# Last stage of a layer kernel: sixteen tokens per partition, loads at the last scatter's landing, four tiles through TensorE

## What is computed

```python
x = x + g1 * rmsnorm(y, norm_post_mix[l])          # called x1 in the kernel
h = rmsnorm(x, norm_pre_ffn[l]) * (1.0 + sc2) + sh2
out = hier_moe(tokens, ...)                        # sum of two experts' rows per token, called ys
x = x + g2 * rmsnorm(out, norm_post_ffn[l])        # the last stage
```

## Time and profile before

| | |
|---|---|
| median of 3 runs | 2342.1 us (2340.84 to 2342.71) |
| the profiled execution | 2340.58 us, its span 2338.9 us |
| mean granted TensorE clock | 0.97 of 2.4 GHz |
| busy share of the span | PE 93%, DVE 60%, ACT 45%, POOL 28% |
| barrier at the end of the experts | 2291.9 us |
| first square, last sum of the last stage | 2296.2 us, 2335.7 us |

### The profile page before, as it was taken

How to read it: one execution, slowest core, us unless ns; L and a number is a source line. 1 busy time by engine, 2 the same in 40 slices (tenths; PEclk the granted TensorE clock), 3 DMA queues, 4 the chain that set the end, 5 groups by cost and what they waited for, 6 DMA issues and landing times. The chain is left out here.

```text
span 2338.9 us, 35385 instructions
## 1 busy us (share of the span) xinstructions
PE 2166.2 (93%) x11602; PEld 1828.4 (78%) x11603; DVE 1401.5 (60%) x2035; ACT 1056.0 (45%) x1518; POOL 651.5 (28%) x648
## 2 busy tenths in 40 slices
PE   8999999999999679997999959999999999999990
PEld 5888888899998668886888847778788888887770
DVE  6322222387654578886566654765767665647876
ACT  4422322243322036664332234755666665547763
POOL 0000000000000658886222232332333333222323
PEclk9999999999999989998999979999999999999995
DMA  8632333546551986665563336998988987868997
GB/s 308 243 102 109 127 151 130 192 156 215 175 172 63 354 327 229 228 220 190 169 214 138 117 117 183 344 291 250 338 261 261 282 269 246 251 173 277 350 351 301
DMA packets 297516, 518.78 MB, mean 222 GB/s; under 512 B 33406, under 2 KB 206022, under 8 KB 292664
## 3 DMA queue, kind: packets, MB, share of 16 engines
q1 hardware_dynamic: 271000, 439.52, 54.9%
q0 software_dynamic: 17216, 44.60, 8.5%
q10 hardware_dynamic: 9216, 33.56, 3.6%
HBM read 397.28 MB, written 129.09 MB: 225 GB/s over the span
## 5 line engine op out<-in xcount | busy, mean ns | idle before, releaser
L2573 DVE TENSOR_TENSOR e_w_low<-e_w_whole,e_w_high 128x2048 fp32r<-128x2048 f32 x192 | 431.1, 2287 | 92.9 <-ACT e_w_high L2525 92.2
L2525 ACT ACTIVATE e_w_high<-e_w_whole 128x2048 fp32r<-128x2048 f32 x192 | 357.6, 1914 | 47.7 <-DMA e_w_whole<-in_moe_w_down_dram 23.7
L2464 PE MATMUL e_pG<-e_w_high,e_xT 128*128 128x512 f32 x768 | 300.0, 391 | 1.2 <-ACT e_xT L2518 1.2
L2465 PE MATMUL e_pG<-e_w_low,e_xT 128*128 128x512 f32 x768 | 299.7, 390 | 0.0
L859 PE MATMUL proj_acc<-w_high,hT_high 128*128 128x512 f32 x672 | 263.9, 393 | 0.0
L859 PE MATMUL proj_acc<-w_low,hT_high 128*128 128x512 f32 x672 | 262.0, 390 | 0.0
L859 PE MATMUL proj_acc<-w_high,hT_low 128*128 128x512 f32 x672 | 261.8, 390 | 0.0
L2473 PE MATMUL e_pY<-e_w_high,e_hT 128*128 128x512 f32 x768 | 225.4, 405 | 17.5 <-ACT e_hT L2537 17.5
L2468 PE MATMUL e_pG<-e_w_high,e_xT 128*128 128x512 f32 x768 | 189.9, 389 | 0.0
L2473 PEld LDWEIGHTS e_pY<-e_w_high,e_hT 128*128 128x128 f32 x768 | 138.2, 190 | 45.6 <-ACT e_hT L2537 20.3
L2464 PEld LDWEIGHTS e_pG<-e_w_high,e_xT 128*128 128x128 f32 x768 | 144.8, 189 | 31.7 <-issue 1.6
(11 more groups left out here) (304 smaller groups left out, 4171.3 us busy)
## 6 DMA issues: line engine op xcount, KB each, us to landing
e_w_whole<-in_moe_w_gate_dram SPq DMA_DIRECT2D x64, 1024.0 KB, 8.2
e_w_whole<-in_moe_w_up_dram SPq DMA_DIRECT2D x64, 1024.0 KB, 11.1
e_w_whole<-in_moe_w_down_dram SPq DMA_DIRECT2D x64, 1024.0 KB
by_token<-tok SPq DMA_DIRECT2D x32, 512.0 KB, 3.0
w_in_raw<-in_w_mod_dram SPq DMA_DIRECT2D x32, 512.0 KB, 4.3
m_tok<-by_token SPq DMA_DIRECT2D x16, 768.0 KB, 5.4
s_kv<-by_token SPq DMA_DIRECT2D x20, 512.0 KB, 5.8
modulated_high<-hT_high SPq DMA_DIRECT2D x9, 1024.0 KB, 3.9
```

The lines of the kernel that those rows point to most:

```text
L2464: nc.tensor.matmul(pG[:, half], xT[:, 0, k], wh[:, half, w], start=(k == 0), stop=False)
L2465: nc.tensor.matmul(pG[:, half], xT[:, 0, k], wl[:, half, w], start=False, stop=False)
L2525: nc.scalar.activation(wh[:, third, part], raw[:, third, part], ACT.Copy).then_inc(whs.sem, 1)
L2573: nc.vector.tensor_tensor(wl[:, third, part], raw[:, third, part], wh[:, third, part].bitcast(F32), ALU.subtract).then_inc(wls.sem, 1)
```

## The change

- Tile t now holds the tokens 16p + t, p being the partition, so that a partition's 16 rows lie one behind the other in memory. `by_rows` makes that view of `ys`, of x1 and of the output. Any set of neighbouring tiles is then one DMA.
- x1 is loaded with 4 DMAs (2 MB each) in place of 16; SyncE does not wait for them, VectorE and TensorE do.
- `c_yy` gets its place ahead of the stage, where the split weights lay. SyncE issues the loads of `ys` at the end of its program in the experts, when GpSimd reports the last scatter landed (`summed_up`): 6 DMAs of 1, 1, 2, 4, 4 and 4 tiles.
- The output goes out in 7 DMAs.
- The tiles 2, 6, 10 and 14 (`by_pe`) are not summed by VectorE. ScalarE makes a diagonal matrix of rstd (`finish`); TensorE adds ident times x1 (done at the stage's start) and the diagonal times the tile in PSUM, in two halves of 512 columns, all in f32; ScalarE copies the sum into `c_yy`. `finish(t - 3)` stands behind the square of tile t for t = 5, 9 and 13, and `finish(14)` at the end.

```diff
--- before.py
+++ after.py
@@ -2264,6 +2264,7 @@
     with ExitStack() as st:
         raw = g["e_raw"]
         kit.fill("e_fill_first", 2048, st)
+        g["c_yy_at"] = nc.sbuf_base
         wh = kit.sb("e_w_high", [P, 3, THIRD], F32R, stack=st)
         wl = kit.sb("e_w_low", [P, 3, THIRD], F32R, stack=st)
         ids = kit.sb("e_ids", [P, IDS], I32, stack=st)
@@ -2301,7 +2302,10 @@
         ya = kit.counter("e_y_act", 1, credit=3)
         yd = kit.counter("e_y_dve", 1, credit=3)
         junk = kit.counter("e_paused")
-        x1_early = kit.landing("c_x1_early_in", dmas=NL)
+        g["x1_early"] = x1_early = kit.landing("c_x1_early_in", dmas=4)
+        g["c_y_in"] = kit.landing("c_y_in", len(LOADS))
+        summed_up = kit.counter("c_rows_summed")
+        g["c_yy"] = kit.at("c_yy", [P, NL, D], g["c_yy_at"])
         block = st.enter_context(nc.Block())
 
         def over_blocks(eng, body, enter=None):
@@ -2349,17 +2353,19 @@
             sp.wait_ge(x_in.sem(0), x_in.at(0))
             with sp.Fori(1, NE // 4) as e:
                 load(e)
-            for t in range(EARLY, NL):
-                sp.dma_start(early_x1(g, t), dram["x1"][t]).then_inc(x1_early.sem(0), 16)
+            sp.dma_start(g["x1_rest"][:], by_rows(dram["x1"].rearrange("t p d -> (t p) d"), EARLY, NL)).then_inc(x1_early.sem(0), 16)
             with sp.Fori(NE // 4, NE) as e:
                 load(e)
 
             for third in range(3):
 
                 sp.wait_ge(wls.sem, wls.at(NE - 1, 2 * third + 2))
-                for t in range(4 * third, 4 * third + 4):
-                    sp.dma_start(early_x1(g, t), dram["x1"][t]).then_inc(x1_early.sem(0), 16)
-            sp.wait_ge(x1_early.sem(0), x1_early.at(0))
+                to = raw[:, third].rearrange("p (t d) -> p t d", t=4)
+                sp.dma_start(to, by_rows(dram["x1"].rearrange("t p d -> (t p) d"), 4 * third, 4 * third + 4)).then_inc(x1_early.sem(0), 16)
+
+            sp.wait_ge(summed_up.sem, summed_up.at(0))
+            for n, (t, last) in enumerate(LOADS):
+                sp.dma_start(g["c_yy"][:, t:last], by_rows(dram["ys"][0:SEQ], t, last)).then_inc(g["c_y_in"].sem(n), 16)
 
         @block.gpsimd
         def _(pool):
@@ -2428,6 +2434,7 @@
                 nc.gpsimd.tensor_copy(held[:, 0:3 - n], held[:, 1:4 - n]).then_inc(held_on.sem, 1)
                 scatter(b + n)
                 landed(b + n)
+            pool.sem_inc(summed_up.sem, 1)
             pool.wait_ge(x_in.sem(0), x_in.at(b))
             pool.sem_inc(junk.sem, 1)
 
@@ -2604,6 +2611,13 @@
 
 
 EARLY = 12
+LOADS = ((0, 1), (1, 2), (2, 4), (4, 8), (8, 12), (12, 16))
+STORES = ((0, 2), (2, 4), (4, 8), (8, 12), (12, 14), (14, 15), (15, 16))
+
+
+def by_rows(rows, t, last):
+
+    return rows.rearrange("(p t) d -> p t d", t=NL)[:, t:last]
 
 
 def early_x1(g, t):
@@ -2618,34 +2632,63 @@
     GROUP = 2
 
     with ExitStack() as st:
-        yy = kit.sb("c_yy", [P, NL, D], stack=st)
+        kit.fill("c_fill_first", 2048, st)
+        assert nc.sbuf_base == g["c_yy_at"]
+        kit.sb("c_yy_room", [P, NL, D], stack=st)
+        yy = g["c_yy"]
         sq = kit.sb("c_sq", [P, D], stack=st)
         ss = kit.sb("c_ss", [P, 2, NL], stack=st)
-        y_in = kit.landing("c_y_in", NL)
-        o_out = kit.landing("c_out", dmas=NL)
+        diag = kit.sb("c_diagonal", [P, NL // 4, P], stack=st)
+        pS = kit.ps("c_sums", [P, NL // 4, 2, 512], st)
+        y_in = g["c_y_in"]
+        x1_early = g["x1_early"]
+        o_out = kit.landing("c_out", dmas=len(STORES))
         ssq = kit.counter("c_ssq")
         eps_added = kit.counter("c_eps_added")
         rstd = kit.counter("c_rstd")
         gained = kit.counter("c_rows_gained")
+        diags = kit.counter("c_diagonal_ready")
+        summed = kit.counter("c_sums_ready")
         outs = kit.counter("c_out_ready")
+        outs_pe = kit.counter("c_out_of_sums_ready")
         block = st.enter_context(nc.Block())
+
+        def by_pe(t):
+
+            return t % 4 == 2
+
+        def before(t, kind):
+
+            return sum(by_pe(n) == kind for n in range(t))
 
         @block.sync
         def _(sp):
-            for t in range(NL):
-                sp.dma_start(yy[:, t], dram["ys"][t * P:(t + 1) * P, :]).then_inc(y_in.sem(t), 16)
-            for t in range(NL):
-                sp.wait_ge(outs.sem, outs.at(t))
-                sp.dma_start(io["out0"][0, t * P:(t + 1) * P, :], yy[:, t]).then_inc(o_out.sem(0), 16)
+            to = by_rows(io["out0"].rearrange("o n d -> (o n) d"), 0, NL)
+            for t, last in STORES:
+                sp.wait_ge(outs.sem, before(last, False))
+                if before(last, True):
+                    sp.wait_ge(outs_pe.sem, before(last, True))
+                sp.dma_start(to[:, t:last], yy[:, t:last]).then_inc(o_out.sem(0), 16)
             sp.wait_ge(o_out.sem(0), o_out.at(0))
 
         @block.scalar
         def _(act):
-            for t in range(NL):
-                act.wait_ge(y_in.sem(t), y_in.at(0))
-                if t:
-                    act.wait_ge(ssq.sem, ssq.at(t - 1))
-                nc.scalar.activation(sq[:], yy[:, t], ACT.Square, accum_out=ss[:, 0, t:t + 1]).then_inc(ssq.sem, 1)
+            def finish(t):
+                n = before(t, True)
+                act.wait_ge(rstd.sem, rstd.at(t // GROUP))
+                nc.scalar.activation(diag[:, n], g["ident"][:, :], ACT.Copy, scale=ss[:, 1, t:t + 1]).then_inc(diags.sem, 1)
+                act.wait_ge(summed.sem, summed.at(n))
+                nc.scalar.activation(yy[:, t], pS[:, n].rearrange("p a b -> p (a b)"), ACT.Copy).then_inc(outs_pe.sem, 1)
+
+            for n, (t0, last) in enumerate(LOADS):
+                act.wait_ge(y_in.sem(n), y_in.at(0))
+                for t in range(t0, last):
+                    if t:
+                        act.wait_ge(ssq.sem, ssq.at(t - 1))
+                    nc.scalar.activation(sq[:], yy[:, t], ACT.Square, accum_out=ss[:, 0, t:t + 1]).then_inc(ssq.sem, 1)
+                    if t >= 5 and by_pe(t - 3):
+                        finish(t - 3)
+            finish(NL - 2)
 
         @block.gpsimd
         def _(pool):
@@ -2654,6 +2697,22 @@
                 span = slice(n * GROUP, (n + 1) * GROUP)
                 rstd_root(nc, g, pool, eps_added, n, 1, ss[:, 1, span], ss[:, 0, span], D).then_inc(rstd.sem, 1)
 
+        @block.tensor
+        def _(pe):
+            pe.wait_ge(x1_early.sem(0), x1_early.at(0))
+            for t in range(NL):
+                if by_pe(t):
+                    for h in range(2):
+                        nc.tensor.matmul(pS[:, before(t, True), h], g["ident"][:, :], early_x1(g, t)[:, h * 512:(h + 1) * 512], start=True, stop=False)
+            for t in range(NL):
+                if by_pe(t):
+                    n = before(t, True)
+                    pe.wait_ge(gained.sem, gained.at(t))
+                    pe.wait_ge(diags.sem, diags.at(n))
+                    for h in range(2):
+                        m = nc.tensor.matmul(pS[:, n, h], diag[:, n], yy[:, t, h * 512:(h + 1) * 512], start=False, stop=True)
+                    m.then_inc(summed.sem, 1)
+
         @block.vector
         def _(dve):
             def gain(t):
@@ -2662,9 +2721,12 @@
 
             for t in range(GROUP):
                 gain(t)
+            dve.wait_ge(x1_early.sem(0), x1_early.at(0))
             for t in range(NL):
                 if t + GROUP < NL:
                     gain(t + GROUP)
+                if by_pe(t):
+                    continue
                 dve.wait_ge(rstd.sem, rstd.at(t // GROUP))
                 dve.wait_ge(gained.sem, gained.at(t))
                 nc.vector.scalar_tensor_tensor(out=yy[:, t], in0=yy[:, t], scalar=ss[:, 1, t:t + 1], in1=early_x1(g, t), op0=ALU.mult, op1=ALU.add).then_inc(outs.sem, 1)
```

## The result

The changed kernel takes 2347.5 us (median of 20 runs, 2344.4 to 2351.4), the kernel before 2342.4 (20 runs beside it): ratio 1.0019, 95% interval 1.0011 to 1.0027, so about 4.4 us slower (the medians lie 5.1 apart). Run again later (e10_again) it gave 1.0014 (1.0004 to 1.0023). The difference is small, but the interval leaves out 1, so it is a measured one. The profiled execution took 2351.39 us, its span 2349.4.

A forecast was written before the change was run, and what follows sets the result against it. VectorE was taken to set the kernel's end; after the change ScalarE's chain of squares, finishes, root and tail would end at 2341.3 against 2338.9, +2.4 us. On the median 2342.1 + 2.4 = 2344.5 us, range 2337.5 to 2350.

The forecast's parts named there:

- The early loads: Last stage: loads issued at about 2287.5, ScalarE starts 4.1 us earlier; SyncE being held bounded at +1.3 on tile 4.
- The group of tile 4: Last stage: tiles 4 to 7 land together at 2300.6; ScalarE waits for tile 4 until then, not 2297.1.
- One finish: ScalarE's diagonal 0.47, TensorE's products 3.8, PSUM copy 1.03, handovers 0.15: 5.45 us at the lower clock, 3.7 at the higher.
- The clock: TensorE in the last stage: higher clock (2.4 GHz) for the first finish, lower (1.2 GHz) for the other three.
- lower clock for the first as well: Rival: TensorE at the lower clock for the first finish too; +1.75, so +4.2, 2346.3 us; chance 0.2.
- the higher one throughout: Rival: TensorE stays at the higher clock, all four finishes at 3.7 us; -2.8, 2339.3 us; chance 0.2.
- The last root: GpSimd's root for the last pair, ahead of the finish of tile 14: 2.25 us, done at 2332.2.
- The tail: Behind the last PSUM copy: 3.2 us of store and end, plus 0.4 for tile 15's store issued behind tile 14's.
- Strided rows: Rival, loads of `ys`: reads 64 KB apart run at half rate, ending at 2353, +14; chance 0.05.
- The packets of x1: Rival: 16 KB packets of x1 land the last-but-one scatter 4.3 us later, the last scatter 1.2 later; chance 0.15.
- Hidden, at nothing: x1 in 4 DMAs instead of 16, ahead of the last stage: costs no time, save for the rival on packets.
- "Below" the forecast: Range's lower end, 2337.5: all finishes at the higher clock less 2 us for earlier landings; over 0.2% faster had chance 0.1.

The follow-up runs named there:

- e10_again: The changed kernel as it is, run once more: stage 61.97 us, ratio 1.0014 (1.0004 to 1.0023) to the kernel before.
- e3_early_only: The kernel before with only its sixteen tile loads of `ys` issued early, in the old layout: stage 61.09 us, ratio 1.0011 to the kernel before.
- e7_loads_by_tile: The changed kernel with its early loads of `ys` as 16 DMAs of one tile: stage 66.25 us, one execution, 2350.34 us.
- e2_pe_busy: The changed kernel with six unread TensorE products behind each of the first three sums: stage 56.72 us, ratio 1.0002 to the kernel before.
- e4_apart: The changed kernel with each PSUM copy four squares behind its diagonal, and tiles 1, 5, 9, 13 by TensorE: stage 54.38 us, ratio 0.9974 to before.

## Why the prediction held, and which steps did not

Forecast 2344.5 us with a range of 2337.5 to 2350, no measurable change the likeliest. Measured 2347.5; the last stage +2.65 us where +2.4 was forecast. "No measurable change" is not what came out: I took 0.2% as the least that can be told, but the interval is 0.08% to either side, and 1.0019 is a real loss. It lies within the 0.2% that I gave the best chance. That the stage is so near is luck in part. Tile 4 (0.7 us) and the finishes of tiles 2 and 14 (0.4 and 0.3) came in under the forecast, the roots (0.6 at the last one, 0.3 net at the two before) and the tail (0.7) over it. The working against the trace, in us behind TensorE's end in the experts:

| step | forecast | measured |
|---|---|---|
| loads of `ys` issued | 7.9 | 7.78 |
| first square | 12.4 | 12.66 |
| tile 4 begun | 21.0 | 20.28 |
| finish of tile 2 over | 27.1 | 25.96 |
| finish of 6 over | 37.5 | 36.52 |
| finish of 10 over | 47.9 | 47.07 |
| last diagonal | 52.6 | 52.38 |
| last copy over | 58.1 | 57.57 |
| end of the span | 61.7 | 61.91 |

- **The early loads**: right, and nothing was held at SyncE, as taken. The bound that I kept for SyncE being held is what sixteen loads do (e3_early_only, e7_loads_by_tile): 18.4 and 17.3 us to the first square.
- **The group of tile 4**: right in kind, 0.7 us early.
- **One finish**: 5.45 us forecast at the lower clock. Diagonal, wait, copy up to the next square took 2324.01 - 2318.76 = 5.25, so 0.2 less. It hides a term that I left out: ScalarE also waited 0.57 and 0.56 us for GpSimd's root ahead of the second and the third sum.
- **The clock**: first sum at the higher one, three at the lower, as taken from rows 11 and 12, and shown by e2_pe_busy. The rivals "lower clock for the first as well" and "the higher one throughout" are both out. But the way to it was narrow. I had the rise 3 to 4 us after the products with x1 begin and 2.5 us between their end and the first finish; the rise came after 6.0 us, they took 10.1 us, and 0.15 us were left. In e7_loads_by_tile nothing was left, and the first finish waited for them.
- **The last root**: 2.25 us forecast, 2.99 waited. Mis-sized: GpSimd's add took 1.25 us, not the 0.55 of the earlier trace rows (below).
- **The tail**: 3.6 us forecast behind the last copy, 4.3 measured. The grouped stores have landed by then; the last two stores go 0.4 us apart, and the second takes 3.4 us to land, where I had 2.6.
- **Strided rows**: that rival is out, 21.1 us for the last group.
- **The packets of x1**: the rival's mechanism is real, 3.4 us (11.55 - 8.14) where it had 4.3, and so it fell just inside the slack and not 1.2 us beyond it. But "Hidden, at nothing" is the step that failed, at another place: the 2 MB load in the middle of the experts, of which I worked out nothing, holds up the gather of the next tokens by 3 us and the experts by about 2 us. Of that 0.8 remain at their end by the profiles, and some 1 to 2 by the medians. That is about what the measured 3.3 and 4.4 us have over the 2.65 of the stage.
- **"Below" the forecast**: a faster result needed earlier landings or the higher clock. It was the order on ScalarE that would have brought it. VectorE lost 4.7 us of work, but ScalarE took over the waiting: 13.8 us behind TensorE. With diagonal and copy apart this falls to one wait.
- **"ScalarE's own work"**: the 39 us of the forecast are work and waits together. Four diagonals and four copies add 4 x (0.40 + 1.02) = 5.7 us of work to the 20 of the squares; the rest of the growth is idle time, and that is why another order could take it away.

## What to carry to other kernels

Work moved off the engine that bounds a stage should not be waited for by an engine that others depend on: give the order to start it early and fetch its result some items later, and the slow clock of a mostly idle TensorE costs nothing here. Loads that are issued ahead of a barrier must be few enough for the queue's engine to be through by then. Large transfers save issues, but they delay other queues' small ones (a gather or scatter of 0.5 MB by 3 us here), and at a stage's end they delay the last landing. And a term put at nothing should be looked for at every place where the change makes it, also far ahead of the stage in question.

## What was not expected of the hardware

GpSimd's add of two columns (L214) takes between 0.18 and 1.25 us in the kernels before and after, and it ends with a VectorE instruction. Two of these adds in the changed kernel, and VectorE's instruction at the time of the last:

```profile
2305.70 0.19 POOL L214 TENSOR_TENSOR c_ss<-c_ss,eps 128x2 f32<-128x2 f32 x1
...
2336.96 1.25 POOL L214 TENSOR_TENSOR c_ss<-c_ss,eps 128x2 f32<-128x2 f32 x1 [5.34 <-ACT c_sq L2688]
```
```profile
2336.88 1.28 DVE L2732 SCALAR_TENSOR_TENSOR c_yy<-c_yy,c_ss,x_rest 128x1024 f32<-128x1024 f32 x1
```

The second ends at 2338.21, 0.05 us behind the VectorE instruction that had begun 0.08 before it (2338.16). So do seven of the eight adds in this trace, and seven of the eight in that of before: each ends 0.04 to 0.06 us after a VectorE instruction. The eighth begins while VectorE is idle, and takes 0.19. The power that follows takes 1.55 us in most rows, but 0.73 when it begins in a pause of VectorE, and up to 3.88 beside its instructions. Two powers of e4_apart:

```profile
2300.35 0.73 POOL L216 TENSOR_TENSOR c_ss<-c_ss,neghalf 128x2 f32<-128x2 f32 x1
...
2319.60 3.88 POOL L216 TENSOR_TENSOR c_ss<-c_ss,neghalf 128x2 f32<-128x2 f32 x1
```

The second of these is what ScalarE waits 1.49 us for at its diagonal of tile 13. This is read from the rows, not tried by itself. The Trainium skill (SBUF — State Buffer, "SBUF: two separate sides") has the two engines share a pair of ports that one of them holds for a whole instruction, also when VectorE's has two inputs in SBUF and GpSimd's reads SBUF. GpSimd's rows agree. That VectorE is ever held up by GpSimd they don't show: its instructions beside the powers of the changed kernel take their usual 1.22 to 1.28 us. An add at the wrong moment costs up to 1.1 us more (1.25 - 0.19). In the changed kernel that is the whole wait of 0.57 and 0.56 us at the second and third finish, and 1.1 of the 2.99 at the last.

Most of SyncE's issues of these loads take 0.32 to 0.50 us, but one or two at the end of sixteen take 1.05 to 1.43 (before, e3_early_only) or 1.20 (e7_loads_by_tile). In all, sixteen loads take 10 us (e3_early_only), six with the same bytes 2.8. What makes the last ones long was not tried.
